# An S5 mixer prologue reordered: norm weight at the evictions, two table tiles, memory products spread differently, input loads on another queue

## The reference, cut to what matters

```python
hn = rmsnorm(h, mix_norm[0])                      # x * rsqrt(mean(x^2)+eps) * g
# s5_mixer(hn): 64 groups of 16 channels, 64 complex states each
bu     = einsum('blgc,gpc->blgp', u, b_bar)       # inflow
states = associative_scan(s[t] = lam_bar*s[t-1] + bu[t])
y      = real(einsum('blgp,gcp->blgc', states, c)) + d_skip*u
z      = gelu(y);  zw = z @ w_glu                 # 1024 x 2048
h      = h + zw[:, :D] * sigmoid(zw[:, D:])
...
# later layer, needs only the inputs mem and w_mem_kv
kv = rms_norm(mem, norm_mem_g) @ w_mem_kv         # 256 x 1024 @ 1024 x 2048
```

## Time and profile before

| | us |
|---|---|
| median of three runs (lowest, highest) | 2356.22 (2353.73, 2358.70) |
| the profiled execution, whole | 2351.14 |
| its span in the trace | 2349.4 |
| PE busy | 2286.8 (97%) |
| DVE, ACT, POOL busy | 1397.8, 898.3, 205.5 |
| start of the first product of `glu` | 173.18 |
| mean granted clock of TensorE | 0.993 of full |

### The profile page before, as it was taken

The page is one execution under the profiler, slowest core; times in us unless marked ns, Lnnn a source line. Parts: engine busy times, 40 slices in busy tenths (PEclk is TensorE's granted clock), DMA queues, the critical chain, the costliest instruction groups (busy, mean ns, idle before and its releaser), DMA issues.

```text
span 2349.4 us, 29568 instructions
## 1 busy us (share of the span) xinstructions
PE 2286.8 (97%) x10720; PEld 1888.7 (80%) x10720; DVE 1397.8 (59%) x1966; ACT 898.3 (38%) x1348; POOL 205.5 (9%) x152
## 2 busy tenths in 40 slices
PE   6989999999999999999999999999999999999999
PEld 5977788888788878888887788887887888888887
DVE  7864554544888876544446657775355657644443
ACT  3323332222476743222244535554344543322221
POOL 6502300000300031000020000002000003000000
PEclk9999999999999999999999999999999999999999
DMA  6373222222221112222222222113222122222222
GB/s 218 61 193 106 90 98 98 99 95 93 92 73 60 63 68 90 98 98 98 97 92 79 73 81 70 57 63 126 98 90 90 68 76 98 91 98 99 99 93 86
DMA packets 79988, 218.41 MB, mean 93 GB/s; under 512 B 18576, under 2 KB 28048, under 8 KB 79376
## 3 DMA queue, kind: packets, MB, share of 16 engines
q1 hardware_dynamic: 72704, 208.37, 26.8%
q10 hardware_dynamic: 7184, 8.68, 1.1%
HBM read 206.40 MB, written 6.29 MB: 91 GB/s over the span
## 4 chain that ended last, share of the span: by engine, by line
PE 88%; DVE 4%; ACT 4%; DMA 1%; SPq 1%; issue 1%; ACTq 0%; DVEq 0%
PE lin L469 26%; PE lin L471 26%; PE lin L470 26%; PE tr L513 1%; PE tr L693 1%; SPq L352 1%; ACT w_hi L969 1%; DVE w_lo L1395 1%; PE sc L552 1%; PE tr L815 1%; PE sc L679 1%; DMA ssm_u<-x_a 0%; PE sc L680 0%; PE tr L528 0%; PE tr L870 0%
## 5 line engine op out<-in xcount | busy, mean ns | idle before, releaser
L969 ACT ACTIVATE w_hi<-w_raw 128x1024 fp32r<-128x1024 f32 x353 | 374.1, 1060 | 1021.8 <-PE lin L471 1018.6
L469 PE MATMUL lin<-x_hi,w_hi 128*128 128x512 f32 x1472 | 592.9, 403 | 3.2 <-DVE x_lo L1400 1.6
L471 PE MATMUL lin<-x_hi,w_lo 128*128 128x512 f32 x1472 | 574.1, 390 | 0.0
L470 PE MATMUL lin<-x_lo,w_hi 128*128 128x512 f32 x1472 | 573.8, 390 | 0.0
L1395 DVE TENSOR_TENSOR w_lo<-w_raw,w_hi 128x1024 fp32r<-128x1024 f32 x353 | 450.1, 1275 | 102.5 <-ACT w_hi L969 100.1
L469 PEld LDWEIGHTS lin<-x_hi,w_hi 128*128 128x128 f32 x1472 | 276.8, 188 | 70.2 <-issue 9.8
L470 PEld LDWEIGHTS lin<-x_lo,w_hi 128*128 128x128 f32 x1472 | 276.8, 188 | 64.7 <-issue 9.2
L471 PEld LDWEIGHTS lin<-x_hi,w_lo 128*128 128x128 f32 x1472 | 276.5, 188 | 58.4
L469 PE MATMUL lin<-q_hi,w_hi 128*128 128x512 f32 x688 | 269.4, 392 | 11.2 <-DVE q_lo L1400 9.2
L471 PE MATMUL lin<-q_hi,w_lo 128*128 128x512 f32 x688 | 268.6, 390 | 0.0
L470 PE MATMUL lin<-q_lo,w_hi 128*128 128x512 f32 x688 | 268.6, 390 | 0.0
(11 more groups left out here) (421 smaller groups left out, 2693.3 us busy)
## 6 DMA issues: line engine op xcount, KB each, us to landing
w_raw<-w SPq DMA_DIRECT2D x353, 512.0 KB, 3.2
w_raw<-w_mem SPq DMA_DIRECT2D x16, 512.0 KB, 3.8
ssm_mt<-ssm_kp SPq DMA_DIRECT2D x64, 64.0 KB, 3.0
ssm_u<-x_a SPq DMA_DIRECT2D x1, 2048.0 KB, 11.1
kv_scratch<-mem_stage SPq DMA_DIRECT2D x8, 256.0 KB, 3.8
resid<-x_b ACTq DMA_DIRECT2D x1, 2048.0 KB, 10.0
z_b<-z_scratch SPq DMA_DIRECT2D x4, 512.0 KB, 4.7
out<-resid SPq DMA_DIRECT2D x8, 256.0 KB, 2.1
```

Source lines behind the costliest of these rows:

```text
L469: nc.tensor.matmul(out, WH[:, b, w], xh[:, k, 0:cols], start=(k == 0), stop=False)
L470: nc.tensor.matmul(out, WH[:, b, w], xl[:, k, 0:cols], start=False, stop=False)
L471: last = nc.tensor.matmul(out, WL[:, b, w], xh[:, k, 0:cols], start=False, stop=(k == KC - 1))
L969: nc.scalar.activation(WH[:, b, :], raw[:, r, :], ACT.Copy).then_inc(s_hi, 1)
```

## The change

It touches the prologue alone.

- The norm weight is no longer multiplied into `U` by POOL. It is applied as ACT's per-partition scale when ACT evicts `ssm_wi` and `ssm_kp`; since the weight differs from group to group, an eviction of two 512-wide activations becomes eight 128-wide ones. POOL multiplies the skip weight by it once (`skip_g`).
- `ssm_wt` gets a second tile, so that DVE writes one while PE transposes the other.
- Memory products: 32 ahead of the first transposes, 4 per inflow batch (32), 8, then 8, 8, 8, 0, 0, 0, and 20 + 4 + 8 behind the last eviction of `ssm_kp`, the last 8 behind the first two `outflow`. The PSUM banks of the pairs, the places of `mem_read` on ACT and of the loads and stores on SP follow.
- SP issues `cols`, `b_re`, `b_im` and `vecs`, and, behind the last load of `z_b`, also `x_b` (the residual, 2 MB, formerly issued by ACT ahead of the first gelu). ACT issues `c_re` and `c_im` behind its second activation.
- The first gelu waits for six stores of `mem_stage`, no longer for eight; the last gelu pair stands ahead of the split of the second quarter of `z`.

```diff
-    WT = at("ssm_wt", 32 * KB, [GB, CH, GC])
+    WT = [at("ssm_wt0", 32 * KB, [GB, CH, GC])]
...
+    WT.append(ss("ssm_wt1", GB * CH * GC * 4, [GB, CH, GC]))
...
-        MB_OF = [TR[0], TR[1], TR[0], TR[2], TR[2], SC[2], TR[2], SC[1]]
+        MB_OF = [TR[0], TR[1], TR[2], TR[2], SC[2], TR[2], SC[0], SC[1]]
...
             sp.wait_ge(s_in[0], 16)
+            for dst, name in ((Bre, "b_re"), (Bim, "b_im")):
+                sp.dma_start(dst[:], a[name]).then_inc(s_in[5], 16)
             sp.dma_start(U[:], a["x_a"]).then_inc(s_in[6], 16)
+            sp.dma_start(VECT[:], a["vecs"]).then_inc(s_in[2], 16)
...
-            for p in range(MEM_PAIRS - 3):
+            def mem_next(p):
+
                 for i in range(2):
                     mem_load(RAW + 2 * p + i)
                 mem_store(p)
+            for p in range(4):
+                mem_next(p)
             for b in range(BATCHES):
-                if b == 4:
-                    for i in range(2):
-                        mem_load(MEM_SLABS - 2 + i)
-                    mem_store(MEM_PAIRS - 3)
+                if b in (1, 3):
+                    mem_next(4 + b // 2)
                 sp.wait_ge(s_kd, b + 1)
...
             for h in range(ZP - 2, ZP):
                 z_load(h)
+            sp.dma_start(R[:], a["x_b"]).then_inc(s_in[1], 16)
...
-            memory(48)
-            pe.wait_ge(s_v, 3)
-            memory(16)
+            memory(32)
             pe.wait_ge(s_u, 1)
...
                 transposes(b)
-                memory(2)
+                memory(4)
                 inflow(b - 1)
-            memory(2)
+            memory(4)
             inflow(BATCHES - 1)
...
-            for b, n in enumerate((4, 4, 5, 5, 6, 0)):
+            for b, n in enumerate((8, 8, 8, 0, 0, 0)):
                 kernels(b + 2)
                 memory(n)
                 within(b)
-            pe.wait_ge(s_kp, 2 * BATCHES)
-            memory(6)
+            pe.wait_ge(s_kp, GB * BATCHES)
+            memory(20)
             pe.wait_ge(s_mid, 1)
-            memory(10)
+            memory(4)
             for b in range(2):
                 outflow(b)
+            memory(8)
             within(6)
...
-                for j in range(2):
-                    nc.scalar.activation(WI[b % 2][:, 4 * j:4 * j + 4, :].rearrange("p g n -> p (g n)"), TR[j][:], ACT.Copy).then_inc(s_wi, 1)
+                for g in range(GB):
+                    at_g = b * GB + g
+                    nc.scalar.activation(WI[b % 2][:, g, :], TRP[:, g * P:(g + 1) * P], ACT.Copy, scale=SA["gain"][:, at_g:at_g + 1]).then_inc(s_wi, 1)
...
-            for h in range(ZP - 1):
-                gelus(h)
+            act.wait_ge(s_mst, 16 * (MEM_PAIRS - 2))
+            gelus(0)
+            mem_read(MEM_PAIRS - 1)
+            act.wait_ge(s_mst, 16 * MEM_PAIRS)
+            gelus(1)
+            gelus(2)
             z_split(0)
-            z_split(1)
             act.wait_ge(s_state, len(PARTS) - 1)
             split_hi(Slab(-2, 0, None, 0))
             gelus(ZP - 1)
+            z_split(1)
             split_hi(Slab(-1, 0, None, 0))
...
-                dve.wait_ge(s_wtt, b)
+                if b >= 2:
+                    dve.wait_ge(s_wtt, b - 1)
...
-            pool.wait_ge(s_usq, 2)
-            g_.tensor_tensor(U[:], U[:], SA["gain"].unsqueeze(2).to_broadcast([P, G, NK]), ALU.mult).then_inc(s_ug, 1)
```

More of the change, by code:

```diff
@@ L539, in transposes @@
                 if b == 0:
-                    pe.wait_ge(s_mread, 3)
+                    pe.wait_ge(s_mread, 2)
                 if b:
-                    pe.wait_ge(s_wi, 2 * b)
+                    pe.wait_ge(s_wi, GB * b)
                 for g in range(GB):
-                    last = nc.tensor.transpose(TRP[:, g * P:(g + 1) * P], WT[:, g, :, :].rearrange("p j c -> p (j c)"), ident[:])
+                    last = nc.tensor.transpose(TRP[:, g * P:(g + 1) * P], WT[b % 2][:, g, :, :].rearrange("p j c -> p (j c)"), ident[:])
                 last.then_inc(s_wtt, 1)
             def inflow(b):
-                pe.wait_ge(s_wi, 2 * (b + 1))
+                pe.wait_ge(s_wi, GB * (b + 1))
                 if b:
@@ L992, in _ @@
             act.dma_start(T2[:, 0:5 * G], a["ssm_s"]).then_inc(s_in[0], 16)
[L993 to L998, removed]
             act.wait_ge(s_in[0], 16)
@@ L1004, in _ @@
             nc.scalar.activation(SA["er"], SA["zr"], ACT.Exp).then_inc(s_astep, 1)
+            for dst, name in ((Cre, "c_re"), (Cim, "c_im")):
+                act.dma_start(dst[:], a[name]).then_inc(s_in[4], 16)
             act.wait_ge(s_v, c.up(s_v))
@@ L1064, in kernels @@
                     act.wait_ge(s_mt[b % 2], 16 * CH * (b // 2))
-                for j in range(2):
-                    nc.scalar.activation(KP[0:GC, b % 2, 4 * j:4 * j + 4, CH - 1:, :].rearrange("p g j c -> p g (j c)"),
-                                         SC[j][0:GC, :].rearrange("p (g n) -> p g n", g=4), ACT.Copy).then_inc(s_kp, 1)
+                for g in range(GB):
+                    at_g = b * GB + g
+                    nc.scalar.activation(KP[0:GC, b % 2, g, CH - 1:, :].rearrange("p j c -> p (j c)"),
+                                         SCP[0:GC, g * P:(g + 1) * P], ACT.Copy, scale=SA["gain"][0:GC, at_g:at_g + 1]).then_inc(s_kp, 1)
             for b in range(BATCHES):
                 kernels(b)
-                if b in (3, 6):
-                    mem_read(5 + b // 6)
-            act.wait_ge(s_kd, BATCHES)
-            for i in range(2):
-                act.wait_ge(s_mt[i], 16 * CH * BATCHES // 2)
-            act.dma_start(R[:], a["x_b"]).then_inc(s_in[1], 16)
-            mem_read(MEM_PAIRS - 1)
-            act.wait_ge(s_mst, 16 * MEM_PAIRS)
+                if b in (2, 4):
+                    mem_read(3 + b // 2)
+            mem_read(6)
             def gelus(h):
@@ L2075, in _ @@
                 g_.tensor_tensor(clb, clb, TC[:], ALU.add).then_inc(s_cl, 1)
[L2077 removed]
+            after(g_.tensor_tensor(SA["skip_g"][0:GC], SA["skip"][0:GC], SA["gain"][0:GC], ALU.mult))
+            after(g_.tensor_tensor(DK[0:GC], SA["skip_g"][0:GC].unsqueeze(2).to_broadcast([GC, G, GC]),
                                    ident[0:GC, 0:GC].unsqueeze(1).to_broadcast([GC, G, GC]), ALU.mult))
             for b in range(BATCHES):
[L2080 removed]
+                pool.wait_ge(s_kp, GB * (b + 1))
                 lag0 = KP[0:GC, b % 2, :, CH - 1, :]
```

26 lines of the change are left out of this document (12 added, 14 removed).

## The result

| | before | after |
|---|---|---|
| median of 20 runs each | 2355.95 us (2349.43 to 2358.84) | 2360.92 us (2355.05 to 2363.58) |
| the profiled execution | 2351.14 us, span 2349.4, clock 0.993 | 2362.98 us, span 2361.3, clock 0.989 |

After stands to before as 1.0019, interval 1.0012 to 1.0026. The change costs 5.0 us of medians, 0.2%: surely not faster, and so near the bound of 0.2% that the interval holds both sides of it. That says little for the rival: its condition, no fall of the clock at the transposes, held in two of eight profiles only, as told further down.

What follows compares the result with a forecast made beforehand. PE, 97% busy and dense from `glu` on, bounds the kernel, so only `glu`'s start counts. Terms -9.1, +13.2, +6.9, -6.2 give +4.8, with the clock's 3.0 +7.8: 2356.2 + 7.8 = 2364 us, range 2353 to 2373.

Steps and rivals of the forecast that it cites:

- the rival: At the second transposes: PE's clock does not fall, so +4.8 in all, 2361 us; chance 0.25.
- start and inflow: Prologue up to `kernels`: transposes start 13 us earlier, `kernels` at 80.5 against 89.61, -9.1 us.
- the clock's fall, once: At the second transposes: PE falls to 1.2 GHz after 2.5 us idle, as before, +3.0 us.
- Toeplitz leg: From `kernels` to the last `ssm_kp` eviction: SP stands 4.4 and 4.8 us at loads 13 and 15, +13.2 us.
- behind the last eviction, to `outflow`'s end: PE after the last `ssm_kp` eviction: sixteen more products, 7.4 us, less the scan's wait of 0.47, +6.9 us.
- from there to `glu`'s second part: After `outflow`: the last gelus no longer wait for the second quarter of `z`, -6.2 us.
- Norm weight off POOL, second table: Start of prologue: POOL's 7.05 us product goes, DVE's tables up to 7 earlier, worth nothing beyond letting 32 products move.
- Eviction in eight: ACT's evictions: 0.30 us per 128-wide copy, bounds 0.14 and 0.41; 2.5 us in place of 1.1.
- Inflow: Prologue ahead of `kernels`: seven rounds of 4.54 us each, 3.66 plus 0.88 for two more products, PE being full.
- rival of a slower PE: Toeplitz stretch: 1.2 GHz lasts or falls at `kernels(1)` too, 3 to 6 us each; up to +16, 2372; chance 0.15.
- `x_b`: Issued by SP behind the last gelus, there at +16 to +17, needed at +17.0: costs nothing, bounds 0 and 3.
- the rival in which SP doesn't stand: Toeplitz stretch: slabs 9 and 11 multiplied before SP asks, 9.2 us of standing go; 2352 or 2355; chance 0.12.

Runs made afterwards that it cites:

- the last experiment: The changed kernel run once more, unaltered, for a second profile: 2360.70 us, 1.0018 to before.
- the last of the mixed kernels: Changed kernel with SP's load pairs ahead of batches 2 and 4, memory products spread between `kernels`, last memory read ahead of the first gelus: 2344.54 us, 0.9950.

## Why the prediction was right, and where its terms were off

The sum was in four terms, with a fifth for the clock. "First" is the changed kernel's profile above, "second" the last experiment's; all against before.

| term | forecast | first | second |
|---|---|---|---|
| start and inflow (`kernels` at) | -9.1 | 80.22 - 89.61 = -9.4 | 79.53 - 89.61 = -10.1 |
| the clock's fall, once | +3.0 | 0 | 1.7, within the row above |
| Toeplitz leg | +13.2 | 59.00 - 44.18 = +14.8 | 59.06 - 44.18 = +14.9 |
| behind the last eviction, to `outflow`'s end | +6.9 | 36.67 - 30.21 = +6.5 | 36.66 - 30.21 = +6.5 |
| from there to `glu`'s second part | -6.2 | 14.88 - 20.52 = -5.6 | 14.09 - 20.52 = -6.4 |
| sum | +7.8 | +6.25 | +4.8 |

The medians say +5.0, and the prediction had 173.2 + 4.8 = 178 for `glu`'s first product, which came at 177.63. The mechanism was the one foretold: 9 us gained ahead of `kernels`, lost in SP's queue, and a net loss of the products that had been cover and now lie behind.

- *Norm weight off POOL, second table:* worth nothing by themselves, each shown by a run of its own; for POOL's product the prediction said so.
- *`x_a`:* +0.9, as said.
- *Eviction in eight:* 0.27 each on 128 partitions (2.17 / 8) and 0.26 on 16 (2.11 / 8), where I had taken 0.30 between 0.14 and 0.41. The Trainium skill's price (ScalarE: Activation LUTs, What ACT_TABLE_LOAD costs), an estimate of 0.29 here, was nearer. With about four of them on the path and 0.2 to 0.3 each, this was 1 us too much, by estimate.
- *Inflow:* a round takes 4.34, not 4.54. The two products more in a round added 0.84, near the 0.88 that was counted (1.73 instead of 0.89); but the 3.66 was not all PE's own work, it was the time of three DVE instructions of 1.22 each: with DVE out of the way transposes and inflow take 0.16 less in a round. In seven rounds the 0.20 by which a round is shorter are 1.4; with one wait of 0.39 for an eviction and the transposes 0.5 later than forecast (`x_a`'s sums took 10.2) `kernels` were 0.3 earlier than 80.5. (The sentence on the eviction ahead of the transposes names rows 2 for the pause of 0.78; it is the earlier trace rows.)
- *The clock* is the term that failed. In size: one fall cost 1.7 in the second execution, not 3.0. Before's profile stayed at 1.2 GHz (a granted clock of 0.50) from about 59.5 to 66.3, twice as long as the second execution did (43.4 to 46.8), and I took its whole cost for that of one fall. In kind: I made it a property of the place. Of the eight profiles with the new order of the start (the two above among them), six have it at the second transposes and two have not; five have it at `kernels(1)`. With SP's order of the changed kernel, the leg took 59.0 and 59.1 where it fell at `kernels(1)`, and 56.4 and 56.9 where it did not: the 1.6 by which `kernels(2)` come later come back as 2.1 to 2.6. SP carries them: from the start of `kernels`, load 13 goes out 1.6 later in the first two profiles than in the others (17.2 against 15.5) and load 15 2.1 later (36.0 against 34.0). I had this place in the rival of a slower PE, at a price of 3 to 6. The page TensorE: Matmul & The Clock Gate of the Trainium skill (Why this matters for your kernels), by which idle gaps let the clock drop, agrees with the direction these rows show; the gaps that it speaks of are longer than the 2.29 and 2.36 here, and by these rows shorter ones do it too.
- *Toeplitz:* +13.2 became +14.8. Load 13 held SP until 97.38 (forecast 96.2) and load 15 until 116.34 (113.9), late by the falls at `kernels(1)` and at 109.04, where `kernels(4)` took 3.50. SP stood 5.3 and 5.9 us for them, forecast 4.4 and 4.8, and 1.4 more for load 12, which the working had without a wait. The last eviction ended at 139.17, forecast 137.8. Both stands were where they had been put.
- *Sixteen more products behind:* +6.5 for +6.9, 24 of the 32 products in one piece, and no wait of PE for the scan. With 16 behind the eviction again, in the last of the mixed kernels, this stretch took 29.52 (162.56 - 133.04) instead of 36.67.
- *Last gelus:* they begin 0.4 ahead of `outflow`'s end, forecast 0.8 behind it. The order itself is worth 3.3 to 4 by the profiles; its two runs gave 3.9 and 1.6 in the medians. The rest, 20.52 - 17.40 = 3.1, is there in the changed kernel with the old order: the second quarter's split begins 1.7 behind `outflow`'s end (175.34 against 173.65), before 5.0. I put that down to the products that now stand ahead of `outflow`'s end and give `z` time to get ready; no run takes it apart.
- *`x_b`:* it was issued at 181.42 and took 9.6, so it was there at 191.0. DVE took up `val` at 194.21 and waited for PE: nothing, as said. The working of this term did not add up: an issue 11 us behind the last gelus and 10.0 to land are +21, past the +17.0 at which DVE needs it, and not the +16 to +17 given. The term came out because the issue stood only 6.0 behind the gelus (181.42 against 175.46).

```profile
181.42 0.47 SPq L422 DMA_DIRECT2D resid<-x_b  x1
...
194.21 1.14 DVE L1582 COPY val<-lin 128x512 f32<-128x512 f32 x1 [6.09 <-PE lin L478]
```

(Timelines of SP and DVE in the changed kernel.) So the forecast came 3 us too high. Up to `kernels` it was 3.3 and 4.0 too high in the two executions, by the clock's term (3.0 and 1.3 of it) and by the start and the rounds; the Toeplitz leg, in which it counted no fall, gave 1.6 and 1.7 back. That these errors have opposite signs is luck. A sum of terms this near the limit of what the runs can tell was right in its sign by its largest term, SP standing; the rival in which SP doesn't stand was put at 2352 to 2355, and the run with the later loads gave 2353.8.

## What to carry to other kernels

A load whose buffer is still in use is a promise to wait: if it stands in a queue ahead of transfers that something needs, count back to when its buffer comes free, and put it behind them. Work that is moved forward to fill one gap is missing as cover in the next; the same change with its loads a batch later, its products spread over all `kernels` and the last memory read ahead of the gelus is 0.5% faster than before instead of 0.2% slower. And compare profiles by the stage that was changed, since profiled executions of the same code differ elsewhere by as much as such a change is worth (2164.9 to 2173.2 from the second part of `glu` on).

## What the runs showed of the hardware

- Which idle time of PE is followed by 1.2 GHz changes from one execution to the next of the same program: at the second transposes (idle 2.36) and at `kernels(1)` (idle 2.29) the profiles show both. `keep_clock` inside `glu` took 5.42 behind an idle time of 1.46 in the second execution, and 6.94 behind 1.43 in the run with the loads later.
- The start of the transposes lay between 39.8 and 42.2 us in the eight profiles with the same code up to there, and ACT's squares, which wait for `x_a`, began between 14.6 and 15.4.
- Small DVE instructions that begin beside one of POOL's products last until it ends. Timelines of the changed kernel, DVE and then POOL:

```profile
67.09 1.98 DVE L1529 COPY acc<-lam_im 64x64 f32<-64x64 f32 x1
69.08 0.19 DVE L1530 TENSOR_SCALAR acc<-lam_im 64x64 f32<-64x64 f32 x1
69.30 1.94 DVE L1534 TENSOR_TENSOR acc<-acc 128x64 f32<-128x64 f32 x1
```

```profile
66.98 2.04 POOL L2073 TENSOR_TENSOR ssm_cl<-c_re,pow_x 128x1024 f32<-128x1024 f32 x1
```

An instruction of DVE that falls together with one of POOL ends with it, about 2 us later; the next, in POOL's gap, takes 0.2. It was off PE's path here.
